# A hybrid decoder trunk on one core: the recurrence's root taken by tokens, one low weight part made by GpSimd, a rejoined opening and TensorE fillers

## What is computed

```python
h = rms_norm(x, norm_mix[l]); u = h @ w_in[l]              # 1024 x 2412
y_a = mla_mixer(u[..., :o1], ...)                          # latent attention
y_b = nsa_mixer(u[..., o1:o2], ...)                        # compressed, selected and window attention
y_c = rglru_mixer(u[..., o2:o3], ...)                      # gated linear recurrence over the tokens
y_d = ssd_mixer(u[..., o3:], ...)                          # Mamba-2 state space, ends in its own rms_norm
y = concatenate([rms_norm(y_a, g[0]), rms_norm(y_b, g[1]), rms_norm(y_c, g[2]), y_d])
x = x + y @ w_out[l]; h = rms_norm(x, norm_ffn[l])
x = x + (swiglu(h, ...) if l == 0 else moe_ffn(h, ...))    # dense 3584 wide; top 2 of 8 experts
```

## Time and profile before

| | |
|---|---|
| runs (median, range) | 1519.4 us (1519.02 to 1522.42) |
| the profiled execution: its own time, its span | 1522.7 us, 1520.8 us |
| TensorE busy | 1487.0 us of the span, 98% |
| VectorE, ScalarE, GpSimd busy | 1218.0, 1004.1, 77.5 us |
| mean granted TensorE clock | 0.995 |
| DMA | 444 MB, 292 GB/s on average |

### The profile page before, as it was taken

One profiled execution on the slowest core, in us unless ns is written; L12 is line 12 of the kernel. 1 busy time (PEld: TensorE's weight loads), 2 busy tenths in 40 slices (PEclk: granted clock), 3 DMA queues, 4 the chain that ended last, 5 costly groups with the idle time before them and its releaser, 6 DMA issues.

```text
span 1520.8 us, 19966 instructions
## 1 busy us (share of the span) xinstructions
PE 1487.0 (98%) x7379; PEld 1246.2 (82%) x7379; DVE 1218.0 (80%) x1279; ACT 1004.1 (66%) x890; POOL 77.5 (5%) x124
## 2 busy tenths in 40 slices
PE   7999999999999999999999999999999999999997
PEld 6987888888798788878888888888888888888885
DVE  6678644544667889998899889888989889889986
ACT  6476544333547677777777777777777778778764
POOL 3101000000000020000000000000000000000000
PEclk9999999999999999999999999999999999999998
DMA  9804655555440269999999999999999999999991
GB/s 318 246 1 128 220 190 176 194 188 191 167 139 1 84 244 393 396 343 394 394 352 388 394 364 377 396 389 349 394 395 346 394 396 342 395 397 346 393 396 76
DMA packets 189963, 444.22 MB, mean 292 GB/s; under 512 B 9713, under 2 KB 15998, under 8 KB 189902
## 3 DMA queue, kind: packets, MB, share of 16 engines
q1 hardware_dynamic: 185350, 427.81, 76.7%
q0 software_dynamic: 4528, 15.58, 3.9%
q10 hardware_dynamic: 24, 0.01, 0.0%
HBM read 435.51 MB, written 7.86 MB: 292 GB/s over the span
## 4 chain that ended last, share of the span: by engine, by line
PE 93%; DVE 3%; ACT 2%; issue 1%; DMA 0%; SPq 0%; POOLq 0%; DVEq 0%; POOL 0%; ACTq 0%
PE bank L457 27%; PE bank L458 27%; PE bank L456 27%; PE bank L589 3%; PE bank L515 2%; PE bank L592 1%; PE bank L703 1%; PE bank L751 1%; ACT w_hi L1337 0%; PE bank L761 0%; PE bank L720 0%; PE bank L977 0%; DMA work<-in_nsa_cmp_pe_dram 0%; PE bank L621 0%; ACT work L1493 0%
## 5 line engine op out<-in xcount | busy, mean ns | idle before, releaser
L1822 DVE TENSOR_TENSOR w_lo<-ring,w_hi 128x2048 fp32r<-128x2048 f32 x372 | 846.5, 2290 | 177.0 <-ACT w_hi L1364 176.4
L1364 ACT ACTIVATE w_hi<-ring 128x2048 fp32r<-128x2048 f32 x372 | 712.0, 1916 | 223.3 <-PE bank L456 223.3
L457 PE MATMUL bank<-w_hi,xT_hi 128*128 128x512 f32 x896 | 353.7, 395 | 0.0
L458 PE MATMUL bank<-w_hi,xT_lo 128*128 128x512 f32 x896 | 349.5, 390 | 0.0
L456 PE MATMUL bank<-w_lo,xT_hi 128*128 128x512 f32 x896 | 240.2, 390 | 0.0
L457 PE MATMUL bank<-w_hi,hidT_hi 128*128 128x512 f32 x560 | 220.8, 394 | 2.7 <-DVE hidT_lo L1829 2.7
L458 PE MATMUL bank<-w_hi,hidT_lo 128*128 128x512 f32 x560 | 218.3, 390 | 0.0
L456 PEld LDWEIGHTS bank<-w_lo,xT_hi 128*128 128x128 f32 x896 | 168.2, 188 | 35.7
L458 PEld LDWEIGHTS bank<-w_hi,xT_lo 128*128 128x128 f32 x896 | 168.5, 188 | 33.7
L457 PEld LDWEIGHTS bank<-w_hi,xT_hi 128*128 128x128 f32 x896 | 168.3, 188 | 33.6
L457 PE MATMUL bank<-w_hi,hT_hi 128*128 128x512 f32 (+2 forms) x384 | 149.9, 393 | 6.9 <-DVE hT_lo L1777 2.7
(11 more groups left out here) (386 smaller groups left out, 1261.6 us busy)
## 6 DMA issues: line engine op xcount, KB each, us to landing
ring<-in_moe_w_gate_dram SPq DMA_DIRECT2D x112, 1024.0 KB, 9.4
ring<-in_moe_w_up_dram SPq DMA_DIRECT2D x112, 1024.0 KB, 9.4
ring<-in_moe_w_down_dram SPq DMA_DIRECT2D x112, 1024.0 KB, 9.0
ring<-in_ffn_w_gate_dram SPq DMA_DIRECT2D x14, 1024.0 KB, 5.1
ring<-in_ffn_w_up_dram SPq DMA_DIRECT2D x14, 1024.0 KB, 5.1
ring<-in_ffn_w_down_dram SPq DMA_DIRECT2D x14, 1024.0 KB, 4.8
ring<-in_w_in_dram SPq DMA_DIRECT2D x12, 1024.0 KB, 7.0
ring<-in_w_out_dram SPq DMA_DIRECT2D x8, 1024.0 KB, 8.0
```

Source lines behind the costliest of these rows:

```text
L457: pe.matmul(o, x_hi, w, start=start, stop=False)
L458: return pe.matmul(o, x_lo, w, start=False, stop=False)
L1364: act.activation(w_hi[:, (base + at) % SPLIT, :], ring[:, i, :], ACT.Copy).then_inc(hi_ready, 1)
L1822: dve.tensor_tensor(w_lo[:, v, :], ring[:, (base + at) % RING, :], w_hi[:, v, :].bitcast(F32), ALU.subtract).then_inc(lo_ready, 1)
```

## The change

**Loop end.** `Sqrt` for the recurrence (old L1555) moves from step 6 to step 8 on ScalarE, behind the high parts of outputs 0 and 1. `turned_output` now lies on ScalarE: it reads the turned bank and scales by the gain as it writes the high part; VectorE makes the low part in one operation from the same bank. The plain `yT` of these three groups is not written any more. `lru_square` is turned round, so that tokens lie along partitions and the sums take 4 columns for each block; the root is a GpSimd power of two columns, and `lru_spread` brings it back to channels with two matmuls of a diagonal matrix. Their place is inside `project_output(1)`, before its low part. `split(p + 11)` leaves VectorE for GpSimd. `outputs(6)` moves behind the recurrence. ScalarE's `split(p + 12)` and `split(p + 13)` come forward.

```diff
@@ TensorE
 def lru_square():
-    pe.wait_ge(lru_act, 5 * l + 4)
+    pe.wait_ge(lru_act, 4 * l + 4)
     b = bank(0)
-    for i in range(2):
-        mm = pe.matmul(b[:, 0:S], ones[:, :], lt1[:, i, :], start=(i == 0), stop=(i == 1))
+    for tb in range(TB):
+        for i in range(2):
+            mm = pe.matmul(b[:, 4 * tb:4 * tb + 4], lt1[:, i, tb * P:(tb + 1) * P], ones[:, 0:4],
+                           start=(i == 0), stop=(i == 1))
+def lru_spread():
+    pe.wait_ge(lru_diag, l + 1)
+    b = banks[(mark["lsq", l] - 1) % 4]
+    for tb in range(TB):
+        mm = pe.matmul(b[:, tb * P:(tb + 1) * P], ones[:, :], rdiag[:, tb, :], start=True, stop=True)
+    mm.then_inc(lru_rows, 1)
@@ project_output
-    pe.wait_ge(yT_lo_ready, 4 * l + i + 1)
+    if i == 2:
+        pe.wait_ge(yT_lo_ready, l + 1)
+    else:
+        pe.wait_ge(dve_took, mark["yT", l, {0: 0, 1: 2, 3: 1}[i]])
...
+        if i == 1 and low and tb == 0:
+            lru_spread()
@@ GpSimd, between roots(2, 2) and roots(2)
+p = BASE_MIX[l] + 11
+pool.wait_ge(hi_ready, p + 1)
+pool.wait_ge(lo_ready, p)
+pool.tensor_tensor(w_lo[:, p % SPLIT, :], ring[:, p % RING, :], w_hi[:, p % SPLIT, :].bitcast(F32),
+                   ALU.subtract).then_inc(lo_ready, 1)
+c0 = 4 * (5 * l + 3) + 2
+pool.wait_ge(dve_took, mark["lsq", l])
+pool.tensor_tensor(rstd[:, c0:c0 + TB], stat[:, c0:c0 + TB], minus_half[:, 0:TB], ALU.pow)\
+    .then_inc(lru_root, 1)
@@ ScalarE, n == 6, 7, 8
-        act.wait_ge(lru_vec, 4 * l + 3)
-        act.activation(lb[:, :, :], lb[:, :, :], ACT.Sqrt).then_inc(lru_act, 1)
         split(p + 10)
+    if n == 7:
+        turned_output(0, 0)
+    if n == 8:
+        turned_output(1, 2)
+        act.wait_ge(lru_vec, 4 * l + 3)
+        act.activation(lb[:, :, :], lb[:, :, :], ACT.Sqrt).then_inc(lru_act, 1)
         split(p + 11)
         act.wait_ge(lru_vec, 4 * l + 4)
         act.activation(lt1[:, :, :], lgate[:, :, :], ACT.Square, scale=GW ** -0.5).then_inc(lru_act, 1)
-        act.wait_ge(dve_took, mark["lsq", l])
-        act.activation(lrstd[:, :], lrstd[:, :], ACT.Sqrt).then_inc(lru_act, 1)
@@ VectorE, n == 8 and 9
-        split_output(0)
-        turned_output(3)
+        turned_output(0)
         split(p + 10)
-        split_output(1)
-        dve.wait_ge(lru_act, 5 * l + 3)
+        dve.wait_ge(lru_act, 4 * l + 3)
...
-        split(p + 11)
+        outputs(6)
+        turned_output(1)
         b = filled()
-        empty_bank(dve.tensor_scalar(lrstd[:, :], b[:, 0:S], EPS, None, ALU.add))
+        c0 = 4 * (5 * l + 3) + 2
+        empty_bank(dve.tensor_scalar(stat[:, c0:c0 + TB],
+                                     b[:, 0:4 * TB].rearrange("p (t q) -> p t q", t=TB)[:, :, 0], EPS, None, ALU.add))
+        dve.wait_ge(lru_root, l + 1)
+        for tb in range(TB):
+            ins = dve.tensor_scalar(rdiag[:, tb, :], ident[:, :], rstd[:, c0 + tb:c0 + tb + 1], None, ALU.mult)
+        tell(ins, "lru_diag", lru_diag)
     if n == 9:
-        dve.wait_ge(lru_act, 5 * l + 5)
-        link(dve.reciprocal(lrstd[:, :], lrstd[:, :]))
+        dve.wait_ge(lru_rows, l + 1)
```

```diff
@@ TensorE
+            warm_up(4)
...
-            pe.wait_ge(x_in, 16 * TB)
...
-            pe.wait_ge(consts_ready, 1)
-            pe.wait_ge(prow_in, 16 * N_PROW)
...
@@ by_token
                         mm.then_inc(units_used, 1)
+                        if p == 0 and h == 0:
+                            turn_parameters()
@@ ScalarE
+            act.wait_ge(ident_ready, 1)
+            act.activation(stat[:, 3:4], ident[:, 0:1], ACT.Copy)
...
-                    split(p)
+                    split_first()
                     split_turned(0, (2, 3))
+                    split(p + 1)
                     for tb in range(TB):
                         mean_square(0, tb, xres[:, tb, :], D, hn[:, tb, :])
-                    split(p + 1)
```

**Fillers.** Each turn of the overflow loop at the end gets one idle matmul on TensorE:

```diff
             with pe.Fori(0, 3) as o:
+                pe.matmul(banks[0][:, 0:2 * P], ident[:, :], cbias[:, :], start=True, stop=True)
                 with pe.If(novf_r > o):
```

More of the change, by code:

```diff
@@ L283, in trunk @@
         slot_full = [sem(f"slot_full{i}") for i in range(RING)]
-        x_in, prow_in, mixw_in, misc_in = sem("x_in"), sem("prow_in"), sem("mixw_in"), sem("misc_in")
+        x_in = [sem(f"x_in{tb}") for tb in range(TB)]
+        prow_in, mixw_in, misc_in = sem("prow_in"), sem("mixw_in"), sem("misc_in")
+        first_in, first_hi = sem("first_in"), sem("first_hi")
         late_in = sem("late_in")
@@ L429, in turn_sums, with warm_up @@
                             turn_half(norm, b[g], tb, g)
+            def warm_up(times):
+                for _ in range(times):
+                    pe.matmul(banks[5][:, 0:P], ident[:, :], ident[:, :], start=True, stop=True)
             pe.wait_ge(ident_ready, 1)
+            warm_up(4)
             pe.wait_ge(mix_in, 16)
@@ L435, in _, with turn_parameters @@
             give(pe.transpose(b_mix[:, 0:KT], prow[0:KT, 0, :], ident[0:KT, 0:KT]), 0)
-            pe.wait_ge(x_in, 16 * TB)
             mark["raw", 0] = gave[0]
-            for g in range(4):
-                b_x = bank(0)
+            for half in range(2):
+                b_x = [bank(0), bank(0)]
                 for tb in range(TB):
-                    turn_half(0, b_x, tb, g)
-            pe.wait_ge(consts_ready, 1)
-            pe.wait_ge(prow_in, 16 * N_PROW)
[L444 to L451, removed]
+                    if half == 0:
+                        pe.wait_ge(x_in[tb], 16)
+                    for i in range(2):
+                        turn_half(0, b_x[i], tb, 2 * half + i)
+            warm_up(2)
+            def turn_parameters():
+                pe.wait_ge(consts_ready, 1)
+                pe.wait_ge(prow_in, 16 * N_PROW)
+                b_par = banks[7]
+                for l in range(L):
+                    pe.transpose(b_par[:, l * P:(l + 1) * P], prow[:, l, :], ident[:, :])
+                for l in range(L):
+                    for c in range(2):
+                        at = 2 * P + (2 * l + c) * (CLEN // 2)
+                        mm = pe.transpose(b_par[:, at:at + CLEN // 2], pe_row[:, l, c, :],
+                                          ident[0:CLEN // 2, 0:CLEN // 2])
+                mm.then_inc(par_turned, 1)
             def products3(o, x_hi, x_lo, w, start, stop, low):
@@ L463, in parts_of @@
                     pe.wait_ge(lo_ready, u0 + (at + 1))
+                elif isinstance(u0, int) and u0 + at == 0:
+                    pe.wait_ge(first_hi, 1)
                 else:
@@ L558, in by_token @@
                             w = parts_of(p, p, h, low).rearrange("p (k n) -> p k n", k=4)
[L559 to L567, removed]
+                            opening = p == 0 and h == 0 and not low
+                            for ks in ((0, 1), (2, 3)) if opening else (range(4),):
+                                if opening and 2 in ks:
+                                    pe.wait_ge(hi_ready, 1)
+                                for tb in range(TB):
+                                    t = slice(tb * P, (tb + 1) * P)
+                                    for k in ks:
+                                        if first and tb == 0 and k % 2 == 0 and not low:
+                                            pe.wait_ge(dve_took, mark["raw", 2 * l] + 2 * h + k // 2 + 1)
+                                        mm = products3(b[tb][:, 0:n], hT_hi[:, 4 * h + k, t], hT_lo[:, 4 * h + k, t],
+                                                       w[:, k, 0:n], h == 0 and k == 0, h == 1 and k == 3, low)
+                                    if h == 1 and low and tb == 0:
+                                        give(mm, 1)
                         mm.then_inc(units_used, 1)
+                        if p == 0 and h == 0:
+                            turn_parameters()
                     filled_by[1].append((units_used, p + 2))
@@ L1326, in _ @@
             act.dma_start(prow[0:KT, :, :], norm_mix.rearrange("l (a b) -> a l b", b=P)).then_inc(mix_in, 16)
-            act.wait_ge(x_in, 16 * TB)
+            act.wait_ge(ident_ready, 1)
+            act.activation(stat[:, 3:4], ident[:, 0:1], ACT.Copy)
+            for tb in range(TB):
+                act.wait_ge(x_in[tb], 16)
             fills = [0] * RING
```

95 lines of the change are left out of this document (58 added, 37 removed).

## The result

| | before | after |
|---|---|---|
| median of 7 runs each (range) | 1520.9 us (1519.0 to 1522.4) | 1526.6 us (1525.7 to 1527.6) |
| profiled execution, its span | 1522.7, 1520.8 us | 1527.4, 1525.6 us |
| TensorE busy | 1487.0 us | 1493.5 us |
| GpSimd busy | 77.5 us | 88.0 us |

The changed kernel is slower by 5.7 us: ratio 1.0038, interval 1.0028 to 1.0047. The forecast was 1510.1 us, with a range up to 1521.5; both are missed, and the sign with them. The forecast counted from the median of three runs, 1519.4; seven runs have it at 1520.9, so 1.5 us of the miss are the base's. TensorE is busy for 6.5 us more.

A forecast was written before the change was run, and what follows sets the result against it. TensorE, 93% of the chain, was taken as the bound, so only its waits and slow stretches could give time. Opening -3.0, two loop ends -6.0 and end -0.3 sum to -9.3 us: 1510.1 us, range 1508.0 to 1521.5.

The forecast's parts named there:

- the hold: Loop end: GpSimd's subtraction and VectorE's operations with two SBUF inputs exclude each other for the whole instruction; chances 0.19 and 0.20.
- The first rival: Each loop end: GpSimd's subtraction holds VectorE behind the scans, then TensorE's clock is low; +2.1 us in all, 1521.5; chance 0.19.
- H: Loop end: duration of GpSimd's subtraction for unit p + 11, taken as 4.3 us, at most 5.1.
- The second rival: Each loop end: VectorE is held, but small matmuls keep TensorE's clock up; -1.3 us in all, 1518.1; chance 0.20.
- the prediction's main case: Whole kernel: VectorE not held, all terms gained; -9.3 us, 1510.1; chance 0.48, including fillers that leave the clock low.
- Loop end: Each of two mixer loop ends: second and third output products start sooner; -3.0 us each.
- Opening: Kernel start: unit 0's low part and the rope arguments come sooner, so TensorE's unit 3 does; -3.0 us, bounds -1.1 and -4.5.
- End: Last eight matmuls: faster clock, mostly hidden by VectorE's additions and ScalarE's squares; -0.3 us, bounds -1 and +0.5.
- the second product ends the slack: Loop end: starting the first output product 2.1 us sooner saves nothing alone, as the second sets the time.

The follow-up runs named there:

- E2: The changed kernel with GpSimd's subtraction cut into four pieces of 512 columns: 1517.62 us, ratio 0.9975.
- E3: The kernel before with one part of the change alone, GpSimd instead of VectorE making unit p + 11's low part: 1531.24 us, ratio 1.0072.
- E6: The changed kernel with GpSimd taking the root first and subtracting after it: 1517.61 us, ratio 0.9979.
- E1: The changed kernel with unit p + 11's low part back on VectorE, GpSimd keeping only the root: 1512.65 us, ratio 0.9946.
- E4: The kernel before with only the new opening: 1518.51 us, ratio 0.9984.
- E8: The kernel before with only one filler matmul in each turn of the last loop: 1519.94 us, ratio 0.9992.
- E9: The changed kernel with 10 idle matmul calls ahead of TensorE's wait for the recurrence's output: 1521.42 us, ratio 0.9999.
- E7: The kernel before with only the new loop end, old opening and no filler: 1528.06 us, ratio 1.0053.

## Why the prediction failed

**The step that failed is a reading of two rows.** The prediction gave the hold a chance of 0.39 in its two rivals together, and set it against the earlier trace rows: "where GpSimd was first, VectorE kept its length". In those rows GpSimd works on one or two columns. They were called weak in the text and then still tipped the scales. So the sum kept 0.69 us for the operation behind the scans, and nothing for a wait on it; it measured 4.89, and TensorE stood still for 4.75. The runs show the hold at length: on four different operations of VectorE (after, E2, E3, E6) and, in E1, on GpSimd's. The Trainium skill's page "SBUF — State Buffer", section "Who interferes with whom", had said it: VectorE with two SBUF inputs and GpSimd reading SBUF exclude each other for the whole instruction, in the order of issue. The traces agree (4.89 for 0.69 behind 4.53; 2.67 for 0.70 behind 2.28), and a rule with a mechanism should have outweighed two rows that could hardly show it. Why the short operations of GpSimd didn't hold VectorE is still open; no run here was made for it.

**The times that led to the collision were right.** Taken back by the opening's 2.7 us, the forecast had GpSimd starting at 127.2 and the scans ending at 127.3; they were 127.35 and 127.50. GpSimd's duration was put at 4.3 us and was 4.53; the Trainium skill's page "GPSIMD Engine Reference", section "Performance versus the Vector engine", gives 4497 ns, and the trace agrees with it. A sum that puts two starts within 0.2 us of each other has found its main risk.

**The first rival was the case, and under-priced.** Its formula gives 4.53 - 3.3 + 1.7 = +2.9 us a loop end; the ruler has +4.2. Two terms were short. The slow matmuls cost 1.8 us in layer 1, which the ruler spans (a high pass of 5.66 us against 3.84), and 2.1 in layer 0 (5.97), instead of 1.7. And the squares and the last step's matmuls ahead of the product, free in the formula, ran at the low clock too: 2.36 us from 133.14 to 135.50, against 1.24 in E1; this 1.1 us is the larger of the two. With 8.4 us for two loop ends, less 2.9 (E4) and 1.2 (E8), the sum is +4.3; measured are +5.7. The second rival, with a clock that stays up because small matmuls lie in the gap, is out: they lie at its end. E9 builds that case: the rival had +1.0 us a loop end, the ruler has +1.4. Against the runs of before taken beside it E9 is 0.5 us faster, where the rival had 1.3; its 1521.4 us against 1518.1 come for the most part from the base, which was 1521.95 in those runs and 1519.4 in the forecast.

**Without the hold the sum was about right.** E1 is the change as the prediction's main case pictured it. Loop end: -3.0 forecast, -2.9 by the ruler. Opening: -3.0 forecast, -2.9 in E4. End: -0.3 forecast, -1.2 in E8. The forecast's sum is -9.3, and E1 measured -8.8 against the runs beside it; its parts as measured apart give -9.9. The term for the end was mis-sized, as far as one pair of profiles shows: I had VectorE's additions hide most of a faster clock, but from the last matmul to the end of the span it is 8.4 us before (1512.39 to 1520.8) and 8.7 after (1516.90 to 1525.6), so all but 0.3 of the 1.23 us came through. In layer 0 the profile of before also ran 1.65 us later to the first turn than E8, which has the same code there (154.20 and 152.55). Eleven matmuls of its product of unit 0 were slow, six in E8's. So the one profile of before flatters the opening: over E8's profile the new opening gains 1.5 us (E4's turn is at 151.05). The medians say 2.9, the ratio 2.4.

**Chances.** Slower by over 0.3% had 0.06, because the first rival's price needed H above 5. With its two missing terms it would have been over the line at the H that was forecast.

## What to carry to other kernels

Before an elementwise job goes to GpSimd, list every VectorE operation that runs beside it and mark those with two inputs from SBUF and those that scale or add to a tensor in SBUF (tensor-scalar): if one of them is on the path, the job isn't free but can cost its whole duration there (4.3 of 4.5 us here, 2.5 where TensorE had other work), and then the low clock of TensorE. Price a gap on TensorE with what follows it (everything up to the point where the clock is back), and prove the clock's share by idle matmuls that fit the gap, counted in trace rows. When a sum shows two engines starting within some tenths of a microsecond of each other, run the change with that one move undone first: here it was worth 13.9 of 1526.6 us.

## What the runs showed that I had not expected

- A tensor-scalar operation with one tensor in SBUF is held as well: 4.81 for 0.48 us in E6. So counting inputs isn't enough. The Trainium skill's page "SBUF — State Buffer", section "Who interferes with whom", lists this kind among those that can take a mode with two ports; the row agrees with that, though no run here shows the mode. The operations with one input from a PSUM bank that ran beside the subtraction in E2 were not held (0.41 and 0.87).
- Some small ones of that kind also stretch, by 0.28 us, beside GpSimd's issuing of DMAs; others don't, and why isn't known. In the kernel before the same three came after GpSimd's last issue and took 0.18 us each. VectorE in the opening of the changed kernel, where GpSimd issues five DMAs from 18.98 to 22.60:

```profile
20.03 0.46 DVE L1816 TENSOR_SCALAR rk<-ang 128x32 f32<-128x32 f32 x1
20.53 0.18 DVE L1817 TENSOR_SCALAR rk<-rk 128x32 f32<-128x32 f32 x1
20.75 0.47 DVE L1818 TENSOR_SCALAR rk<-rk 128x32 f32<-128x32 f32 x1
```

- A gap of about 0.55 us on TensorE left the clock up (E1), one of 1.50 us brought it down (E2), one of 1.69 us ahead of the spread left it up (E6), and so did one of 4.75 us filled with idle matmuls to within 0.43 us (E9). So the length of a gap doesn't settle it. Nor does the code: waits of 1.30 and 1.08 us ahead of the first output product were followed by the low clock in both layers of the profile of before and by the full clock in both layers of E8's, where the loop end is the same. The distances by the ruler are 382.03 and 381.97, so those slow matmuls cost nothing: the second product ends the slack, as the prediction had it. How many matmuls are slow afterwards differed between equal gaps too: ten in the changed kernel, five in E7 (layer 0).
